# The first level's c·x product of the delta-rule inverse: 32 matmuls of 32x32 in place of 16 of 64x32

## The chip, the cores and the metric

The kernel runs on one NeuronCore of a Trainium2 chip. TensorE (PE in the rows) multiplies, VectorE (DVE) and ScalarE (ACT) do the elementwise work, SyncE (SP) issues nearly all transfers. The metric is the device time of one execution in microseconds; smaller is better.

## What is computed

Two transformer-like blocks on 256 tokens of width 1024, in float32. The first block projects its normed input to four mixers (softmax attention with a forget gate, gated delta rule, and two gated linear attentions), then runs a convolutional gated feed-forward; the second block adds a short convolution mixer, a differential attention and two more feed-forwards. The change lies in the gated delta rule, which solves with a unit lower triangular matrix of 64x64 for each of 4 heads x 4 chunks:

```python
def gated_delta_chunked(q, k, v, g, beta):
    ...
    m = jnp.where(strict, jnp.einsum('bhnrd,bhnsd->bhnrs', kb, k) * decay, 0.0)
    t_mat = m + jnp.eye(c, dtype=m.dtype)
    w = lax.linalg.triangular_solve(t_mat, kb * jnp.exp(G)[..., None],
                                    left_side=True, lower=True, unit_diagonal=True)
    u = lax.linalg.triangular_solve(t_mat, v * beta[..., None],
                                    left_side=True, lower=True, unit_diagonal=True)
    ...
```

## The kernel before

**How the matrices lie.** There are 16 triangular matrices (4 heads, 4 chunks of 64 tokens). Two chunks stand above each other on the 128 partitions, so a tile such as `mt_gd` or `c_t` is [128, 8, 64]: 8 units `u`, each with two 64x64 matrices (`rows_of_chunk(c)`, L373). The inverse is built in blocks: `inv` and `inv_t` are [128, 8, 32] and hold, for each of the four `QUARTERS` of 32 partitions (L382), one 32x32 diagonal block of the inverse and of its transpose.

**How the inverse grows.** `gdn_first_inverse` (L2412) and `gdn_first_turned` on VectorE write the inverse of the 2x2 blocks. Then five levels `lv` = 0 to 4 double the block size: 4, 8, 16, 32 and 64. For each level VectorE makes `c_t` by multiplying `mt_gd` with the mask of that level (`packed(lv + 1)`, L2425 and L2438): at level 0 this leaves entries only inside 4x4 blocks on the diagonal. `gdn_cx(lv)` (L971) multiplies `c_t` with `inv` into PSUM bank 2; ScalarE copies the product to `y_gd` (L1706); `gdn_xcx(lv)` (L981) multiplies `y_gd` and `inv_t` both ways into banks 6 and 0 by `block_products` (L964), which takes 8 units x 4 quarters of 32x32; VectorE subtracts the results from `inv` and `inv_t` (L2445). At level 4 the product joins the two halves of 64 and has a form of its own.

**What sets the order.** All engines run orders written out by hand. On TensorE (L1216 to L1220) the two products of each level are separated by a quarter of a projection (`quarter(*fills[...])`), 12 matmuls of 128x256 that need nothing of the inverse, so that the copies of ScalarE and VectorE lie beside them:

```python
            for lv in range(5):
                gdn_cx(lv)
                quarter(*fills[2 * lv])
                gdn_xcx(lv)
                quarter(*fills[2 * lv + 1])
            gdn_solve()
```

Matmuls of this part are issued by the helper `mm` (L534), those of the projections by `add` (L583). One float32 matmul of L534 in the program shows as two MATMUL records in the trace and two weight loads: the 16 of `gdn_cx` as 32 and 32, the 64 of `block_products` twice as 128 and 128.

**The weights** stream through a ring of three buffers (`raw`, split by ScalarE at L1477 into `w_hi`, by VectorE at L2220 into `w_lo`); SyncE refills a buffer when it has been split. The rest of the program (feed-forwards with a hardware loop of 4 rounds each, attention) comes after and isn't touched.

Of the kernel before, what the change touches and what calls it, by code (L numbers as in the profile page):

```python
# [121 lines left out]
def build(nc, weights, small_in, x_in, masks_in, ident_in, channel_in, row_in, w_gk_in, p_in, table_in,  # L122
# [4 lines left out]
    with ExitStack() as ctx:  # L127
        sems = {}

        def sem(name):  # L130
            if name not in sems:
                sems[name] = ctx.enter_context(nc.semaphore(name))
            return sems[name]
# [36 lines left out]
        def place(shape):  # L170
            n = int(np.prod(shape[1:]))
            at = arena["at"]
            arena["at"] += n
            assert arena["at"] <= ARENA, arena
            v = arena_store[0:shape[0], at:at + n]
            if len(shape) == 3:
                v = v.rearrange("p (a b) -> p a b", a=shape[1])
            elif len(shape) == 4:
                v = v.rearrange("p (a b c) -> p a b c", a=shape[1], b=shape[2])
            return v  # L180
# [49 lines left out]
        c_t = place([P, 8, CHUNK])  # L230
        ngd_tri = place([P, 8, CHUNK])
        HALF = CHUNK // 2
        two_blocks = lambda v: [b.rearrange("p u n -> p (u n)").rearrange("p (u n) -> p u n", n=HALF) for b in (v[:, 0:4, :], v[:, 4:8, :])]
        inv, inv_t = two_blocks(dec)
# [139 lines left out]
        def rows_of_chunk(c):  # L374
            return slice(c * CHUNK, (c + 1) * CHUNK)
# [6 lines left out]
        QUARTERS = [slice(HALF * q, HALF * (q + 1)) for q in range(4)]  # L382

        def block_at(b, u, rows):

            return PS[rows, b, u * HALF:(u + 1) * HALF]
# [145 lines left out]
        def _(pe):  # L532
            def mm(o, lhs, rhs, start=True, stop=True):
                return pe.matmul(o, lhs, rhs, start=start, stop=stop)  # L534
# [436 lines left out]
            def gdn_cx(lv):  # L971

                pe.wait_ge(sem("inv_ready"), lv + 1)
                pe.wait_ge(sem("ct_ready"), lv + 1)
                for u in range(8):
                    for c in range(2):
                        r = rows_of_chunk(c)
                        last = mm(block_at(2, u, r), c_t[r, u, :], inv[r, u, :])
                last.then_inc(sem("cx"), 1)
# [236 lines left out]
# [5 lines that stand above are left out]
# [2192 lines left out]
```

## Time and profile before

| | |
|---|---|
| time, median of 3 runs | 1030.57 us (1029.82 to 1030.59) |
| the profiled execution | 1031.03 us, its span 1029.2 us |
| TensorE matmul busy | 1006.5 us, 98% of the span |
| VectorE busy | 845.6 us, 82% |
| ScalarE busy | 621.4 us, 60% |
| TensorE share of the chain that ended last | 87% |
| granted TensorE clock, mean | 0.998 |
| the stretch from the first `gdn_cx` to the end of the last `gdn_xcx` | 68.97 to 95.6 us |

The page gives each engine's busy time over the span; the chain that ended last gives, followed back from the last instruction, what each step waited for. The clock stood at its upper level (2.4 GHz) in the whole stretch of the change. Instructions are counted as they were executed, the loops' rounds each time.

### The profile page before, as it was taken

The page shows a single profiled execution, that of the slowest core. Times are in us where ns is not written, and L with a number is a line of the kernel's source. Part 1 is how long each engine was busy: PE and PEld are TensorE (multiplying, and loading weights), DVE is VectorE, ACT ScalarE, POOL GpSimd, SP SyncE. Part 2 cuts the span into 40 slices and gives each one's busy share as a digit, 9 for nine tenths or more (in the row PEclk, how much of TensorE's full clock was granted, in tenths as well). Part 3 has the DMA queues.
Part 4 walks back from the last instruction along what each step waited for, and adds up shares of the span by engine and source line. Part 5 has one row for each costly group of instructions (what it writes and reads, how often), then busy time and mean ns, then how long its engine had stood idle before and what let it go on. Part 6 is the DMA issues. An engine that isn't in the chain of part 4 may idle for free.

```text
span 1029.2 us, 21310 instructions
## 1 busy us (share of the span) xinstructions
PE 1006.5 (98%) x8589; PEld 941.0 (91%) x8589; DVE 845.6 (82%) x1211; ACT 621.4 (60%) x856; POOL 5.8 (1%) x16
## 2 busy tenths in 40 slices
PE   7999999999999999999999999999999999999996
PEld 6999889998999999899999999998999999999985
DVE  5964797699988878878999888799775899988876
ACT  6754555566655655556665555666576666555665
POOL 0000000000000000000000000000000000000000
PEclk9999999999999999999999999999999999999999
DMA  8533223455655544566556555444434355655531
GB/s 325 181 100 110 83 85 123 149 193 194 215 188 184 199 163 166 178 232 219 185 205 216 186 204 169 159 164 164 159 130 144 126 202 197 212 187 185 199 123 41
DMA packets 26500, 176.02 MB, mean 171 GB/s; under 512 B 3229, under 2 KB 3509, under 8 KB 6080
## 3 DMA queue, kind: packets, MB, share of 16 engines
q1 hardware_dynamic: 25616, 171.31, 47.8%
q0 software_dynamic: 816, 3.73, 1.1%
q8 instruction: 52, 0.85, 0.3%
q14 instruction: 16, 0.13, 0.0%
HBM read 173.97 MB, written 2.63 MB: 172 GB/s over the span
## 4 chain that ended last, share of the span: by engine, by line
PE 87%; DVE 6%; ACT 3%; DMA 2%; issue 1%; SPq 0%; DVEq 0%; ACTq 0%
PE PS L583 74%; PE PS L534 13%; DVE w_lo L2220 2%; ACT w_hi L1477 1%; DMA arena<-masks_in 1%; DMA raw<-weights 1%; PE PS L1385 0%; DVE h_store L3145 0%; DVE arena L2357 0%; DVE arena L2617 0%; DVE h_store L2233 0%; DVE act_lo L2233 0%; DVE arena L2766 0%; DVE x L2770 0%; PE PS L801 0%
## 5 line engine op out<-in xcount | busy, mean ns | idle before, releaser
L583 PE MATMUL PS<-h_store,w_hi 128*128 128x512 f32 (+1 forms) x1808 | 482.9, 342 | 10.3 <-DVE w_lo L2272 7.5
L2220 DVE TENSOR_TENSOR w_lo<-raw,w_hi 128x2048 fp32r<-128x2048 f32 x156 | 357.1, 2290 | 58.0 <-ACT w_hi L1477 52.8
L583 PE MATMUL PS<-h_store,w_lo 128*128 128x256 f32 (+1 forms) x1384 | 373.3, 282 | 0.0
L583 PEld LDWEIGHTS PS<-h_store,w_hi 128*128 128x128 f32 x1808 | 305.7, 188 | 51.7 <-DVE w_lo L2272 7.8
L1477 ACT ACTIVATE w_hi<-raw 128x2048 fp32r<-128x2048 f32 x156 | 297.8, 1910 | 75.7 <-PE PS L583 60.7
L583 PEld LDWEIGHTS PS<-h_store,w_lo 128*128 128x128 f32 (+1 forms) x1384 | 256.5, 189 | 0.8 <-issue 0.6
L583 PE MATMUL PS<-act_hi,w_hi 128*128 128x256 f32 x704 | 196.4, 281 | 0.2
L583 PE MATMUL PS<-act_hi,w_lo 128*128 128x256 f32 x704 | 195.4, 279 | 0.0
L583 PE MATMUL PS<-act_lo,w_hi 128*128 128x256 f32 x704 | 192.1, 279 | 0.0
L583 PEld LDWEIGHTS PS<-act_hi,w_hi 128*128 128x128 f32 x704 | 132.5, 188 | 2.9 <-issue 1.3
L583 PEld LDWEIGHTS PS<-act_hi,w_lo 128*128 128x128 f32 x704 | 132.5, 188 | 0.0
L583 PEld LDWEIGHTS PS<-act_lo,w_hi 128*128 128x128 f32 x704 | 130.6, 188 | 0.0
L1904 ACT ACTIVATE arena<-PS 128x512 f32<-128x512 f32 x51 | 30.2, 592 | 87.3 <-PE PS L583 87.3
L1896 ACT ACTIVATE arena<-arena,channel 128x256 f32<-128x256 f32 x132 | 63.7, 531 | 22.4 <-DVE arena L2919 15.6
L583 PE MATMUL PS<-w_hi,h_store 128*128 128x256 f32 (+1 forms) x352 | 76.7, 307 | 0.0
L2896 DVE SCALAR_TENSOR_TENSOR arena<-arena,channel 128x254 f32<-128x254 f32 x132 | 57.9, 480 | 7.6 <-DVE arena L2892 0.3
L583 PEld LDWEIGHTS PS<-w_hi,h_store 128*128 128x128 f32 x352 | 57.7, 188 | 3.5 <-issue 0.4
L2892 DVE SCALAR_TENSOR_TENSOR arena<-arena,channel 128x255 f32<-128x255 f32 x132 | 57.7, 479 | 3.8 <-ACT arena L1896 3.8
L583 PE MATMUL PS<-w_lo,h_store 128*128 128x256 f32 (+1 forms) x176 | 52.5, 301 | 0.0
L2917 DVE TENSOR_TENSOR arena<-PS,arena 128x512 f32<-128x512 f32 x51 | 35.0, 687 | 20.6 <-ACT arena L1904 20.6
L534 PE MATMUL PS<-h_store,w_hi 128*128 128x256 f32 x288 | 51.3, 280 | 0.1
L534 PE MATMUL PS<-arena 32*32 32x32 f32 (+7 forms) x1548 | 45.0, 222 | 1.2 <-issue 0.4
(365 smaller groups left out, 1118.9 us busy)
## 6 DMA issues: line engine op xcount, KB each, us to landing
raw<-weights SPq DMA_DIRECT2D x155, 1024.0 KB, 4.9
raw<-weights SPq DMA_DIRECT2D x12, 256.0 KB, 3.6
arena<-masks_in SPq DMA_DIRECT2D x1, 1600.0 KB, 12.1
bias_by_key<-bias_by_distance POOLq DMA_DIRECT2D x1, 1536.0 KB, 9.0
x<-x_in SPq DMA_DIRECT2D x4, 256.0 KB, 4.5
raw<-weights SPq DMA_DIRECT2D x2, 512.0 KB, 9.2
arena<-bias_by_key POOLq DMA_DIRECT2D x1, 1024.0 KB, 6.7
result<-arena SPq DMA_DIRECT2D x4, 256.0 KB, 2.1
```

The source lines that it names most:

```text
L534: return pe.matmul(o, lhs, rhs, start=start, stop=stop)
L583: return pe.matmul(o, lhs, rhs, start=start, stop=stop, skip_group_check=True)
L1477: act.activation(w_hi[:, slot, :], raw[:, slot, :], ACT.Copy).then_inc(hi_ready, 1)
L1896: ins = act.activation(dst[:, c, :], src[:, c, :], ACT.Identity, scale=w, bias=b)
L1904: act.activation(low, PS[:, bank:bank + 2, TOK:512], ACT.Copy).then_inc(sem("low_copied"), 1)
L2220: tt(w_lo[:, slot, :], raw[:, slot, :], w_hi[:, slot, :].bitcast(F), ALU.subtract).then_inc(lo_ready, 1)
L2892: stt(y[:, c, 1:TOK], src[:, c, 0:TOK - 1], channel[:, bass.ds(col(1) + c, 1)], y[:, c, 1:TOK], ALU.mult, ALU.add).then_inc(ready[0], 1)
L2896: ins = stt(y[:, c, 2:TOK], src[:, c, 0:TOK - 2], channel[:, bass.ds(col(0) + c, 1)], y[:, c, 2:TOK], ALU.mult, ALU.add)
L2917: tt(z, PS[:, bank:bank + 2, 0:TOK], low, ALU.add).then_inc(sem("parts_added"), 1)
```

## The change

In `gdn_cx`, level 0 alone takes a branch of its own. Where the code before multiplies, for each unit and each chunk, a 64x64 `c_t` with the 64x32 stack of two `inv` blocks (64 rows contracted, 64 output partitions, 32 columns), the new code multiplies for each unit and each quarter the 32x32 diagonal block of `c_t` with the 32x32 block of `inv` (32 rows contracted, 32 output partitions, 32 columns). `at` picks the columns of `c_t` that belong to the quarter. What is left out are products with the off-diagonal 32x32 blocks of `c_t`, which are zero at this level. Destination, semaphores and waits are the same; levels 1 to 4 are the same.

```diff
@@ -973,6 +973,11 @@
                 pe.wait_ge(sem("inv_ready"), lv + 1)
                 pe.wait_ge(sem("ct_ready"), lv + 1)
                 for u in range(8):
+                    if lv == 0:
+                        for i, r in enumerate(QUARTERS):
+                            at = slice(HALF * (i % 2), HALF * (i % 2) + HALF)
+                            last = mm(block_at(2, u, r), c_t[r, u, at], inv[r, u, :])
+                        continue
                     for c in range(2):
                         r = rows_of_chunk(c)
                         last = mm(block_at(2, u, r), c_t[r, u, :], inv[r, u, :])
```

TensorE's program at this place, between the last projection matmuls before the product and the first ones after it; `w_hi`, `w_lo` and `h_store` are a projection's, `arena` holds `c_t` and `inv`:

```order
@@ -312,6 +312,6 @@
 L583 MATMUL PS<-w_lo,h_store 128x256
 L583 MATMUL PS<-w_hi,h_store 128x256
-L534 MATMUL PS<-arena 64x32 [waits ct_ready,inv_ready]
-L534 MATMUL PS<-arena 64x32 x15
+L534 MATMUL PS<-arena 32x32 [waits ct_ready,inv_ready]
+L534 MATMUL PS<-arena 32x32 x31
 L583 MATMUL PS<-w_hi,h_store 128x256
 L583 MATMUL PS<-w_lo,h_store 128x256
```

Nothing else moves; everything that TensorE's program holds after this place stands 16 matmuls, with their weight loads, further back in it. The other engines' programs are the same but for line numbers.

## Rows read from the trace of the kernel before

**Rows 1.** The page: span, busy time and share of each engine.
```profile
span 1029.2 us, 21310 instructions
...
PE 1006.5 (98%) x8589; PEld 941.0 (91%) x8589; DVE 845.6 (82%) x1211; ACT 621.4 (60%) x856; POOL 5.8 (1%) x16
```

**Rows 2.** The page: chain that ended last, shares of the span.
```profile
PE 87%; DVE 6%; ACT 3%; DMA 2%; issue 1%; SPq 0%; DVEq 0%; ACTq 0%
```

**Rows 3.** The chain by time, 64 to 100 us: start us, us, engine and line.
```profile
71.70 1.16 PE PS L534 x79
72.86 0.40 issue
73.26 0.28 PE PS L534 x9
...
85.21 0.53 issue
85.74 1.09 PE PS L583 x8
...
98.93 0.59 ACT arena L1692
```

**Rows 4.** PE in order of time: start us, us, line, operation, records [idle before].
```profile
68.97 1.12 PE L534 MATMUL PS<-arena 64*64 64x32 f32 x32
70.02 0.39 PE L583 MATMUL PS<-w_hi,h_store 128*128 128x256 f32 x1
...
71.63 1.23 PE L534 MATMUL PS<-arena 32*32 32x32 f32 x119
73.26 0.28 PE L534 MATMUL PS<-arena 32*32 32x32 f32 x9 [0.40 <-issue]
```

**Rows 5.** Windows of L534 on PE: us, busy (records), clock, DMA share, GB/s.
```profile
68.97:70.02 1.05, 1.05 (x32) 1.00 0.00 0
...
80.58:81.63 1.05, 1.05 (x32) 1.00 0.30 117
...
92.28:93.33 1.05, 1.05 (x32) 1.00 0.02 8
77.73:78.97 1.24, 1.24 (x128) 1.00 0.01 0
83.23:84.47 1.24, 1.24 (x128) 1.00 0.43 139
89.43:90.67 1.24, 1.24 (x128) 1.00 0.00 0
```

**Rows 6.** DVE and ACT beside levels 0 and 1, in order of time.
```profile
67.29 0.69 DVE L2425 TENSOR_TENSOR arena<-arena 128x512 f32<-128x512 f32 x1 [3.22 <-ACT arena L1692]
...
69.87 0.43 DVE L2433 TENSOR_TENSOR arena<-arena 128x256 f32<-128x256 f32 x1
70.21 2.29 DVE L2220 TENSOR_TENSOR w_lo<-raw,w_hi 128x2048 fp32r<-128x2048 f32 x1
...
73.59 0.42 DVE L2445 TENSOR_TENSOR arena<-arena,PS 128x256 f32<-128x256 f32 x1 [0.16 <-PE PS L534]
...
70.14 0.38 ACT L1706 ACTIVATE arena<-PS 128x256 f32<-128x256 f32 x1 [0.94 <-PE PS L534]
```

**Rows 7.** The page: the queue of instruction transfers, packets and MB.
```profile
q8 instruction: 52, 0.85, 0.3%
```

**Rows 8.** Windows, all engines: us, PE, PEld, DVE, ACT, POOL, clock, DMA share, GB/s.
```profile
70.42:71.88 1.46, 1.46 (x40) 1.33 (x43) 1.46 (x1) 1.46 (x2) 0.00 (x0) 1.00 0.06 11
75.04:76.03 0.99, 0.99 (x33) 0.95 (x32) 0.10 (x1) 0.00 (x0) 0.00 (x0) 1.00 0.06 17
...
73.25:85.73 12.48, 11.95 (x381) 11.12 (x382) 7.08 (x11) 5.49 (x10) 0.00 (x0) 1.00 0.36 108
...
90.90:92.12 1.22, 1.22 (x12) 1.22 (x11) 1.22 (x4) 0.00 (x0) 0.00 (x0) 1.00 0.55 181
...
293.34:326.72 33.38, 33.38 (x227) 30.88 (x226) 28.37 (x35) 19.44 (x23) 0.00 (x0) 1.00 0.55 188
```

## The prediction

> **What bounds the kernel now.** I read the page first: TensorE is busy for 98% of a span of 1029.2 us [rows 1] and has 87% of the chain that ended last [rows 2]. So what shortens TensorE's own work shortens the kernel, and a wait taken off another engine brings nothing. Next I read the chain by time around the change. From 68.97 to 98.9 us it never leaves TensorE, where ScalarE takes it over at 98.93 [rows 3]; up to there a microsecond off TensorE's row is a microsecond off the chain. In it stand two entries "issue", 0.40 us at 72.86 and 0.53 us at 85.21, where TensorE waits for no other engine [rows 3]. They turn out to be larger than, or as large as, all that the change can gain, so they have to be understood too.
>
> **The product itself.** Before, it is 32 records of 64x32 from 68.97, and the next matmul starts at 70.02: 1.05 us, 32.8 ns a record [rows 4, 5]. The trace has the new form already, in the other product of the levels: 128 records of 32x32 with four quarters in the same order take 1.24 us, 9.7 ns a record, three times the same [rows 5]. The new product is 64 such records: 64 x 9.7 ns = 0.62 us. Gain: 1.05 - 0.62 = 0.43 us. Twice as many instructions cost nothing of their own, since the 9.7 ns already hold a weight load for each matmul. The ends are 0 (64 records at half of 32.8 ns) and 0.43; I take 0.43, because the row is of the same shape, count per unit and bank layout.
>
> A row could speak against it: all four quarters write one PSUM bank, where before two row tiles did. In the 1.24 us rows four quarters also write one bank (6, then 0), so these traces show no price for it [rows 5]. The Trainium skill says otherwise (TensorEngine Tiling (Array Packing), Gotcha 1: PSUM Pressure): "Different row tiles cannot access same PSUM bank simultaneously". By that rule the quarters would go one after another and the gain would shrink or turn round; it is a rival below.
>
> **Who waits for the product.** Its result goes to ScalarE's copy, 0.38 us at 70.14 [rows 6], and comes 0.43 us earlier. The product behind it, from 71.63, needs this copy (ready 70.5) and VectorE's result of L2433 (69.87 + 0.43 = 70.30) [rows 4, 6]. Pulled to 71.20 it still finds both, with 0.7 us to spare. Its own results go to VectorE, which is held by the 2.29 us split at 70.21 until 72.4 and reads the second one at 73.59 [rows 6]; the next user on TensorE comes only at 75.08, after 12 projection matmuls. Inputs of the changed product: `c_t` is written at 67.29 + 0.69 = 67.98, a microsecond before use, and is unaffected [rows 6]. No engine is late by this. SyncE's refills follow the splits, which no one moves. So by the matmuls alone the answer is -0.43 us.
>
> **What the 32 more instructions move.** All later code of TensorE stands 64 records further back in its program (32 MATMUL and 32 weight loads). The two "issue" stalls look like waits for code. First, there is a queue of instruction transfers with 52 packets and 0.85 MB, 16.3 KB each [rows 7]. In windows with nothing else on the DMA engines one read is seen: 11 GB/s x 1.46 us = 16 KB from 70.42 to 71.88, and 17 GB/s x 0.99 us = 17 KB from 75.04 to 76.03 [rows 8]. Second, between the restarts after the stalls, 73.26 and 85.74, TensorE ran 381 + 382 = 763 records and some five waits [rows 8]: 768 = 3 x 256. The whole agrees: 2 x 8589 records [rows 1], less nine repeated loop rounds of 453 [rows 8], over 52 packets, is 252 a packet. So I read: code comes in blocks of 256 instructions, the next block is fetched when one is entered, and a block that is run through faster than a fetch takes ends in a stall. This stretch is the fastest in instructions of the program: a run of 256 records in 1.24 us, against 24 in 1.4 us for a projection quarter.
>
> The Trainium skill has this (Runtime: NRT & Kernel Launch, Instruction fetch mechanics: refills in 16 KiB blocks of 256 instructions, the next fetched while the current one is executed), and calls the cost of crossing a border mostly hidden. The two rows of 0.40 and 0.53 us show it unhidden here; by the page's rule alone there would be no such term and the time would be that of the first rival.
>
> **Where the borders fall.** The restart at 73.26 has 9 of the 128 matmuls left [rows 4], so this border stands 238 records into the first 256-record product. Before, the one ahead of it was reached at 70.4, just behind the changed product. After, each border stands 64 records earlier in the code. Counting 256 at a time through the known order (24 records a projection quarter, 64 a `gdn_cx`, 256 a `gdn_xcx`, a wait or two between), with 4.85 ns a record in the products of 32x32 and 16.4 ns in those of 64x32 [rows 5], the times at which TensorE would reach them are:
> - 71 records into the changed product, 68.97 + 0.34 = 69.31; then 174 into the first `xcx`, 71.63 + 0.84 - 0.43 = 72.04. Block length 2.73 us.
> - 59 into the second `xcx`, 77.73 + 0.29 = 78.02 (length near 6, harmless); then 34 into the third `cx`, 80.58 + 0.56 = 81.14. Length 3.12.
> - 201 into the third `xcx`, 83.23 + 0.97 = 84.20. Length 3.06.
> - 86 into the fourth `xcx`, 89.43 + 0.42 = 89.85 (length 5.6, harmless); then 61 into the fifth `cx`, 92.28 + 1.00 = 93.28. Length 3.43.
>
> The sum of the four short ones is 12.34 us. Before, there were two short ones: 70.4 to 72.86, and 83.3 (9 records into the third `xcx`) to 85.21.
>
> **How long a fetch takes from the border.** From start of read to restart: 73.26 - 70.42 = 2.84. From border to start of read there are two kinds. Where the border follows slow matmuls, or a wait, the read starts with it (70.42 against 70.4); in the midst of a burst or after a stall it starts late: 90.90 [rows 8] against a border at about 90.1, and 75.04 against the restart at 73.26. So from border to usable: 2.47 us (83.27 to 85.74) and 2.9 (70.36 to 73.26) seen as stalls, 0.8 + 1.22 + 1.38 = 3.4 built from the read at 90.90, whose read lasts 1.22 and where 73.26 - 71.88 = 1.38 is what lies behind a read, and 1.78 + 0.99 + 1.38 = 4.2 after a restart. The new short blocks begin in bursts, so I take 3.5, and 3.7 for the third, which follows a stall: 14.2 - 12.34 = 1.9 us of stalls, in place of 0.93. Net of the stalls +0.9, net of all +0.9 - 0.43 = **+0.5 us**. The bounds: with 2.9 everywhere only the first block has a shortfall, 0.17, and the sum is -0.43 - 0.93 + 0.17 = -1.2; with 4.0 it is 16 - 12.34 - 0.93 - 0.43 = +2.3. All three feed-forward loops show equal rounds, so I leave them out. Behind 98.9 us I carry the difference through whole, since TensorE stays the bound.
>
> The sum against the profiled execution is 1031.03 + 0.5 = 1031.5 us; that execution is 0.46 above the median of 1030.57, so the median becomes **1031.1 us**. From no change a measurement here can tell about 0.2%, 2.06 us; even the likeliest case lies deep within that.
>
> **The rivals.**
> - *The borders cost the same*: the reads run early enough, or the stalls have another cause that stays in place. Then only the product counts, -0.43, 1030.1 us. For it: the two stalls seen came at 2.5 to 2.9 us from their border, quicker than my 3.5. Against: stalls of the same size would need the same phase. If the stalls went altogether, it is -1.2 to -1.36, 1029.3 us. Chance 0.38 in all.
> - *Row tiles exclude each other in one bank*: the price of a record stays 32.8 ns, so 64 x 32.8 = 2.1 us, +1.05, 1031.6 us. Against it are the rows of 9.7 ns. Chance 0.03.
> - *Slower, by the code fetch*: every short block costs from its border what the one at 73.26 seems to, 4.2 us. Then 16.8 - 12.34 - 0.93 - 0.43 = +3.1, 1033.7 us. It decides, against the 2.06 us, from (12.34 + 0.93 + 0.43 + 2.06)/4 = 3.94 us a block. For it: the read at 75.04. Against: the four other reads seen. Chance 0.05.
> - *The change does nothing*, as when 32x32 records gain nothing over 64x32 for being half as many: 0, 1030.6 us. Chance 0.04.
>
> **How the numbers follow.** The forecast has 0.50: 1031.1, its own range 1030.4 to 1032.2. The range for 8 in 10 takes in the first rival's far end: 1029.4 to 1032.3. Faster by over 0.2% needs under 1028.5 us, which no case gives: 0.02. Slower needs over 1032.6: the third rival and the tail of the forecast, 0.06. Within: 0.92.
>
> **What would show it.** In the changed kernel's trace: 64 records of 32x32 from 68.97 lasting 0.62 us (right) or over 1.0 (the bank). "issue" stalls no longer behind record 238 of the first `xcx` but behind 174, and not at 85.2 but in the third `cx` and the third `xcx`; stalls 0.4 and 0.5 at the old places would refute the code blocks. The first `gdn_solve` matmul, at 97.2 before, tells the net. The prediction is wrong if that moves by under -0.6 or over +1.6, or if the end moves otherwise than it.

## The result, and the profile after

| | before | changed |
|---|---|---|
| median of 22 runs, taken in turn | 1030.58 us (1029.44 to 1032.18) | 1031.97 us (1030.77 to 1035.0) |
| ratio, 95% interval | | 1.0017 (1.0011 to 1.0023) |
| the profiled execution | 1031.03 us, span 1029.2 | 1032.99 us, span 1031.2 |

The change makes the kernel slower by 1.4 us by the medians, 1.75 us by the ratio (0.17%, an interval of 1.1 to 2.4 us). The forecast was +0.5: the right side, and less than half of the size. The profiled execution is 1.0 us slower than the median of its kind, so its rows show the effect larger than it usually is.

The product does nearly what was said of it. These are the windows of L534 in the changed kernel (us, busy, records, clock, DMA share, GB/s), to be laid beside [rows 5]:

```profile
68.27:68.95 0.68, 0.68 (x64) 1.00 0.00 0
76.91:78.15 1.24, 1.24 (x128) 1.00 0.23 66
```

From the start of the product to the next projection matmul it is 0.68 us in place of 1.05: 0.37 gained, where 0.43 was forecast. The difference of 0.06 is the tail of a burst, which 64 records carry as 128 do. The trace of before had this number too: its product of level 4 is 64 records of 32x32, and its window (same columns) is

```profile
94.94:95.62 0.68, 0.68 (x64) 1.00 0.83 253
```

And this is TensorE in order of time, for [rows 4], the product and all lines of it with idle time before them, and what stands just ahead of those (the view ends at 100.4, inside the last line):

```profile
68.27 0.75 PE L534 MATMUL PS<-arena 32*32 32x32 f32 x64
...
70.56 0.94 PE L534 MATMUL PS<-arena 32*32 32x32 f32 x87
72.16 0.56 PE L534 MATMUL PS<-arena 32*32 32x32 f32 x41 [0.66 <-issue]
...
79.75 0.71 PE L534 MATMUL PS<-arena 64*64 64x32 f32 x17
80.63 0.65 PE L534 MATMUL PS<-arena 64*64 64x32 f32 x15 [0.17 <-issue]
...
82.81 1.08 PE L534 MATMUL PS<-arena 32*32 32x32 f32 x100
84.83 0.44 PE L534 MATMUL PS<-arena 32*32 32x32 f32 x28 [0.94 <-issue]
...
92.32 1.11 PE L534 MATMUL PS<-arena 64*64 64x32 f32 x30
94.29 0.24 PE L534 MATMUL PS<-arena 64*64 64x32 f32 x2 [0.86 <-issue]
...
98.37 1.26 PE L534 MATMUL PS<-arena 64*64 64x64 f32 x38
100.32 0.29 PE L534 MATMUL PS<-arena 64*64 64x64 f32 x4 [0.69 <-issue]
```

The stalls stand where the count of 256 instructions put them: behind 87 matmuls (174 records), 17 (34), 100 (201) and 30 (61), with a fifth in the solve products. Before there were two, 0.40 and 0.53 us [rows 3]. The count holds everywhere: with all of TensorE's records counted from the first one of the program (matmuls, weight loads, and the waits and branches of its sequencer), the number of records ahead of a restart is a multiple of 256 and 193 or 194 more. That is so for every wait of TensorE on "issue" of over 0.1 us from the first product to the linear attention, 48 of them in the 18 profiles of this case. All TensorE's waits of the stretch, in one line of the view of waits, 64 to 101 us (engine and line, waited for: us, times, longest):

```profile
PE PS L534 <- issue: 3.3, 5, 0.9
```

To compare profiles I use two measures of my own from the start times of the matmuls: *the stretch*, from the projection matmul just ahead of the first `cx` to the 1620th matmul of the kernel before (in the linear attention, 110.98 us), and *the pauses*, the distances between successive starts in it that exceed 0.3 us, without one of 0.31 that all have. Behind that matmul the rest takes 909.6 to 910.3 us in all profiles but one, with or without the change (910.9 in the changed kernel with cut transfers), so that part is the same. The start of the stretch varies: the changed kernel's profile reached it at 68.06 us, that of before at 68.76, by nothing that the change touches. This is why the two spans differ by 2.0 us and the two stretches by 2.8.

| profile | stretch, us | pauses, us |
|---|---|---|
| before | 42.22 | 0.59 + 0.81 = 1.40 |
| changed | 45.03 | 0.85 + 0.39 + 1.13 + 1.08 + 0.91 = 4.36 |

2.96 more of pauses less 0.37 for the product is 2.59, of 2.81 measured. There is one profile of before, and two more of the changed kernel, below, have far smaller pauses; so a difference between two single profiles says where time goes, and not how much of it the median loses.

### The profile page after: what moved, and what is told of

It is laid out like the page before. It is cut to its first block, busy times and chain, and to the rows that moved or that the text cites. A ratio compares the mean times of both kernels' runs of the same rounds, so it can differ in the third digit from the quotient of the medians.

```text
span 1031.2 us, 21374 instructions
## 1 busy us (share of the span) xinstructions
PE 1006.4 (98%) x8621; PEld 940.2 (91%) x8621; DVE 845.4 (82%) x1211; ACT 621.6 (60%) x856; POOL 5.8 (1%) x16
## 4 chain that ended last, share of the span: by engine, by line
PE 87%; DVE 6%; ACT 3%; DMA 2%; issue 1%; SPq 0%; DVEq 0%; ACTq 0%
PE PS L583 74%; PE PS L534 13%; DVE w_lo L2225 2%; ACT w_hi L1482 1%; DMA arena<-masks_in 1%; DMA raw<-weights 1%; PE PS L1390 0%; DVE h_store L3150 0%; DVE arena L2362 0%; DVE arena L2622 0%; DVE h_store L2238 0%; DVE act_lo L2238 0%; DVE arena L2771 0%; DVE x L2775 0%; PE PS L801 0%
## 5 line engine op out<-in xcount | busy, mean ns | idle before, releaser
L534 PE MATMUL PS<-h_store,w_hi 128*128 128x256 f32 x288 | 51.3, 280 | 0.1
L534 PE MATMUL PS<-arena 32*32 32x32 f32 (+6 forms) x1580 | 45.3, 221 | 4.2 <-issue 3.3
```

## The experiments

**The borders alone.** If it is the place of the code that matters, the kernel before must lose without the new product. The first way used instructions that raise a semaphore:

```diff
+            for _ in range(64):
+                pe.sem_inc(sem('pad'), 1)
             first_columns()
```

> The kernel before, its product unchanged, with 64 instructions that do nothing for the computation (each raises a semaphore that nobody reads) at the start of TensorE's program, where it waits some 7 us for the first inputs. All code behind them stands as far back as in the changed kernel. Theory A (code arrives in blocks of 256 instructions, and the blocks' borders decide): the stalls of the changed kernel without its product: behind 87 of 128 records of the first xcx, 17 of 32 of the third cx, 100 of 128 of the third xcx, 30 of 32 of the fifth cx and in the solve products, 3.0 to 4.4 us in sum in place of 1.4 (start to start), so 1.5 to 3 us slower than before in the profile and +1.8 us (1.2 to 2.5) in the median. Theory B (something about the 32x32 product itself makes the later work late): stalls stay at 119 of 128 and behind the third xcx, and the time is that of before within 0.4 us.

Measured: the stalls moved. The chain of this kernel in order of time (start us, us, what):

```profile
82.75 0.64 PE PS L534 x17
83.39 0.46 issue
83.85 0.65 PE PS L534 x15
...
86.10 1.01 PE PS L534 x69
87.11 0.67 issue
87.78 0.44 PE PS L534 x25
```

Behind 17 of 32 and 100 of 128 records, the changed kernel's places, with the product untouched; none at 119 of the first `xcx` any more. But only two of the five: pauses 1.54, not 3.0 to 4.4; stretch 42.52. The time, 1034.05 against 1030.26 us, is mostly the start: the first matmul came at 10.74 us, not 7.49, since each of these instructions takes some 150 ns (from 128 to 192 of them, below, the first matmul moves by 9.8 us). The 0.5 us left is less than the 1.2 to 2.5 expected. Theory A has the places and not the sizes; theory B has neither.

The same with 16 matmuls of 32x32, 64 records, which are done long before the first input:

```diff
+            pe.wait_ge(*once("zeros"))
+            for i in range(16):
+                r = QUARTERS[i % 4]
+                mm(PS[r, 3, 0:HALF], zeros_r[r, 0:HALF].bitcast(F), zeros_r[r, 0:HALF].bitcast(F))
             first_columns()
```

> The kernel before with 16 matmuls of 32x32 on zeros (64 records) at the very start of TensorE's program, while it waits for its first inputs; they take 0.3 us there and delay nothing, unlike the semaphore instructions that cost 150 ns each. Theory A (borders): stalls at the changed kernel's places, no other difference to before; the profile from the first cx to matmul 1620 between 42.5 (as with 64 semaphore instructions) and 44.7 us, before 42.2; time +0.3 to +1.5 us. If the time is within 0.2 us of before, the phase alone costs nothing and the loss comes from the product's burst.

Measured: first matmul of the kernel proper at 7.19 us, pauses 0.81 and 0.85 at the same two places, stretch 42.64. The median is 1032.73 against 1030.20 us, ratio 1.0026 (1.0013 to 1.0038). More was lost than the 0.3 to 1.5 us expected, 2.5 by the medians (interval 1.3 to 3.9), so about as much as by the change itself or more, in a kernel that has every product as before. Its profiled execution, 1031.29, is the fastest of its six, so the profile shows too little of it; where the other five lost their time isn't seen.

**Back to the old places.** 192 semaphore instructions in the changed kernel, and as controls 128 and 192 in the kernel before:

> The changed kernel with 192 such instructions at the start of TensorE's program: 64 + 192 = 256, so that the borders of blocks fall where they fell before. Theory A: the product at 0.68 us as in the changed kernel (1.05 before), stalls again behind 119 of 128 records of the first xcx and in the projection behind the third xcx, 0.4 and 0.5 us and slightly longer for the 0.37 us that comes earlier; time -0.4 to +0.3 us against before. Should the 192 instructions take longer than the 7 us of waiting at the start, the first matmul is late by it and that is to be taken off. Theory B: as slow as the changed kernel, +1.4 to +1.8 us.

> The kernel before with 128 such instructions: a phase between. Theory A: borders stand behind 55 of 128 records of the first xcx, 110 records (55 matmuls less) earlier in the levels, stalls at other places than in either kernel (in the middle of the second and fourth xcx); their sum between 1 and 4 us, so time -0.4 to +3 us. Theory B: the time of before within 0.4 us.

> The kernel before with 192 such instructions, the control for the 192 of the changed kernel's version: what they cost at the start shows in the first matmul's time. Theory A: stalls at yet other places (third cx and xcx of other levels), sum 1 to 4 us. Theory B: the time of before within 0.4 us.

Measured, the chain of the changed kernel with 192:

```profile
93.41 1.16 PE PS L534 x78
94.57 1.88 issue
96.45 0.28 PE PS L534 x9
...
107.74 0.67 PE PS L583 x4
108.41 1.31 issue
109.72 1.09 PE PS L583 x8
...
122.83 0.80 PE PS L1049 x6
123.64 1.06 issue
124.69 0.44 PE PS L1049 x2
```

The first two are exactly the places of [rows 3], 9 matmuls and 8 projection matmuls ahead of the next piece. Their sizes are not: 1.88 and 1.31 in place of 0.40 and 0.53, and a third has come. The part "borders back, loss back" fails. Medians (1055.47, 1046.52, 1057.51 us) say nothing, since the padding delayed the start to 30.3, 20.5 and 30.3 us. With 128 and 192 in the kernel before, the pauses were 3.01 and 4.20, stretch 43.66 and 45.12: with the old product too, these phases look worse than the one that the kernel before happens to have. These are single profiles, and one and the same kernel ranges from 1.26 to 4.36 (the changed one, below).

**The changed kernel at other phases**, with matmuls as padding, as in the diff above, 16, 32 and 48 of them:

> The changed kernel with the same 16 matmuls at the start: all borders 64 records earlier than in the changed kernel. By block lengths of the changed kernel three blocks are short (2.7, 1.5 and 2.4 us), and at 3.6 to 4.2 us a block the stalls sum to 4.1 to 5.9 us: 1 to 2 us slower than the changed kernel, +2 to +4 us against before. Without theory A: no difference to the changed kernel.

> The changed kernel with 32 such matmuls (128 records) at the start. Short blocks by the changed kernel's lengths: four of 2.9 to 3.25 us, stalls 2.0 to 4.4 us in sum: near the changed kernel, +0.5 to +2.5 us against before.

> The changed kernel with 48 such matmuls (192 records) at the start: 64 + 192 = 256, so borders at the places in the code where they were before, and no late start as with the semaphore instructions. Stalls behind 119 of 128 records of the first xcx, in the projection behind the third and perhaps in the solve. Theory A as first put (the phase of before gives back before's stalls): -0.4 to +0.3 us. As the run with 192 semaphore instructions suggests (the read starts later behind the faster product): stalls 3.2 to 5 us in sum, +1.5 to +3 us.

| padding of the changed kernel, records | ratio to before (interval) | stretch, us | pauses, us |
|---|---|---|---|
| 0 | 1.0017 (1.0011 to 1.0023) | 45.03 | 4.36 |
| 64 | 1.0018 (1.0008 to 1.0027) | 41.81 | 1.53 |
| 128 | 1.0045 (1.0027 to 1.0064) | 43.36 | 2.81 |
| 192 | 1.0014 (1.0003 to 1.0025) | 43.86 | 3.41 |

Again the places held (with 192: 1.63 us idle ahead of 9 matmuls, 1.30 ahead of 8 projection matmuls). With 64 the expectation was too high: 4.1 to 5.9 us of stalls and +2 to +4 us, against 1.53 and +1.6 by the medians. With 128 it was too low: +0.5 to +2.5 us, against +3.3. With 192 the first form of theory A (-0.4 to +0.3) fails, and the median, +1.5, stands at the low end of the second form. The profiles with 64 and 128 are the fastest of their ten and six executions, so they show too little, and the two right columns don't rank the phases. None of the four phases of the changed kernel is as fast as the kernel before. Why the old places cost more with the new product is seen at the first border: it falls 6 or 7 records behind it. In the kernel before the read of the next block began within 0.1 us of TensorE's reaching the border [rows 8]; behind the faster product it began 1.37 and 1.38 us after. TensorE's records then came at three times the rate. The other traces go with this (those with doubled transfers, below, left aside). At the border in or just behind the product, the read began 0.7 to 1.4 us late in all eight profiles in which 71 or more records of the new product had run ahead of it (the three of the changed kernel, cut transfers, even code, four levels, and both with 192 of padding). It began within 0.2 us in the five without: before, before with 64 of padding in both forms, before with cut transfers, and the changed kernel with 64, where the border falls only 7 records into the new product. The last one differs from the changed kernel in its padding alone. How the burst delays the read isn't shown.

**More of the same.** The edit is one line:

```diff
-                    if lv == 0:
+                    if lv < 4:
                         for i, r in enumerate(QUARTERS):
```

> The changed kernel with the product in 32x32 tiles at all of the levels 0 to 3, not at level 0 alone (at these levels too the off-diagonal 32x32 blocks that are left out are zero). By the matmuls alone it takes off 4 x 0.37 = 1.5 us against before, 1.1 against the changed kernel. Theory A: it adds 192 more records, so that a level is 432 records in some 5.1 us, 256 in 3.0 us, below what a block costs (3.5 us and more): the stretch becomes bound by code reads. Stretch from the first cx to the solve: 8.2 blocks at 3.6 to 4.2 us = 29.5 to 34 us against 28.3 before; +1 to +5 us against before. If the bank were the reason of any loss, its record pitch in the levels would be well over 9.7 ns.

Measured: 1036.12 against 1030.14 us, ratio 1.0056 (1.0040 to 1.0073), a little above the range expected. The four products are each 0.37 us shorter, 1.5 in all, and the kernel is 6 us slower. The chain:

```profile
76.62 1.21 PE PS L534 x81
77.83 2.44 issue
80.28 0.32 PE PS L534 x3
...
91.07 0.77 PE PS L534 x55
91.84 1.40 issue
93.24 0.66 PE PS L534 x45
```

The stretch from the first `cx` to the solve was 31.7 us against 28.3, inside the expected 29.5 to 34; the records kept their pace, 64 in 0.68 us and 128 in 1.24. This is the clearest run for theory A: with more instructions for less work the kernel is slower. Part of it is the clock, below.

**Even code.** The projection matmuls in pieces of 6, 12 and 6:

```diff
-                quarter(*fills[2 * lv])
-                gdn_xcx(lv)
-                quarter(*fills[2 * lv + 1])
+                eighth(*fills[2 * lv], 0)
+                gdn_xcx(lv, lambda: (eighth(*fills[2 * lv], 1), eighth(*fills[2 * lv + 1], 0)))
+                eighth(*fills[2 * lv + 1], 1)
```

> The changed kernel with the projection matmuls between the products dealt out finer: 6 ahead of the first 64 matmuls of an xcx, 12 between its two halves, 6 behind, in place of 12 and 12; the same instructions, no data of the one needed by the other. Theory A: code runs more evenly, every block of 256 takes 3.4 to 4.4 us of work; stalls shrink to under 2.5 us in sum, so -1 to -2 us against the changed kernel, if the 6 matmuls (0.7 us) still cover ScalarE's copy of 0.38 us; if they don't, 0.1 to 0.3 us a level are given back. A theory in which the stalls have nothing to do with the rate of instructions: no gain.

Measured: the stalls are gone; from 68 to 99 us the chain has one "issue" entry left, in front of these matmuls (0.23 us from start to start):

```profile
81.36 0.01 issue
81.37 0.65 PE PS L534 x15
```

The blocks took 3.71 to 4.34 us each. The stretch is 42.15 us, which is that of before, and the median 1031.21 against 1030.14, ratio 1.0011 (1.0001 to 1.0020): by the medians 0.8 us less than the changed kernel, but the intervals of the two ratios overlap, so the gain is likely and not shown. The 1 to 2 us expected did not come, and it is not faster than before. What it gives back is the price of changing between 128x128 matmuls and small tiles. Going in there are 0.21 us between starts; coming out 0.12 to the first projection matmul and 0.22 from it to the second, where projection matmuls stand 0.12 apart and records of 32x32 0.01. Two pieces of 6 projection matmuls take 1.82 us where one of 12 took 1.61, and two of 64 small ones 1.36 where one of 128 took 1.24. That is 0.3 us for each of the four levels in which the finer order has one more such pair, 1.3 us, about what the stalls had cost.

**Weight traffic.** The trace records when each read of 16 KB began and ended. In the changed kernel:

| border reached, us | read began | weights arrived | block usable |
|---|---|---|---|
| 68.57 | 69.46 (+0.89) | none | 72.15 (+3.58) |
| 77.14 | 77.92 (+0.78) | 76.3 to 77.7 | 80.63 (+3.49) |
| 80.63 | 82.44 (+1.81) | 79.4 to 80.8 | 84.84 (+4.21) |
| 89.83 | 91.58 (+1.75) | 90.3 to 91.6 | 94.29 (+4.46) |
| 94.29 | 98.13 (+3.84) | 93.4 to 94.8, 95.1 to 98.6 | 100.32 (+6.03) |

In the last three blocks the read began late, in the last two within 0.5 us of the end of a transfer. From the read's end to the next start of a matmul it was 1.24 to 1.51 us in all five. A window in that last wait shows what filled the DMA engines (columns as in [rows 8]: 0.97 of their time, 339 GB/s):

```profile
95.10:98.10 3.00, 3.00 (x84) 2.83 (x84) 0.65 (x2) 0.00 (x0) 0.00 (x0) 1.00 0.97 339
```

So the transfers of blocks 9 to 14 were cut in both kernels (the rest of each buffer keeps older data, so the mixers compute with other numbers), then doubled in both. In both forms blocks 12 and 13 came whole:

```diff
-                sp.dma_start(raw[:, n % RING, :], weights[n - 1]).then_inc(raw_loaded[n % RING], 16)
+                w = 32 if 9 <= n <= 14 else BLK
+                sp.dma_start(raw[:, n % RING, 0:w], weights[n - 1][:, 0:w]).then_inc(raw_loaded[n % RING], 16)
```

> The changed kernel with the transfers of weight blocks 9 to 14 cut to 32 of their 2048 columns (the rest of each buffer keeps older data, so the mixers and projections compute with other numbers; every instruction is as before, and blocks 12 and 13 come in one transfer, not four). It takes nearly all weight traffic out of 70 to 105 us. Theory C (the read of a code block queues behind weight traffic): each read starts within 1.4 us of its border, where 1.8, 2.2 and 3.8 us were seen in the changed kernel; blocks are usable 3.2 to 3.8 us after the border, the stalls at the same five places sum to 1 to 2.3 us (start to start) in place of 4.4, and the time is 2 to 3 us below the changed kernel's, near 1029.5. Theory D (the delay of the reads has nothing to do with weights): stalls sum to about 4.4 again and the time is 1032.

> The kernel before with the same cut in the transfers of weight blocks 9 to 14 (other numbers in the mixers, same instructions). Theory C: its two stalls began without traffic at their reads (read 0.06 us after and 0.38 us before the border), so they stay at 1.4 us in sum within 0.5; time 1030 to 1030.6, and against it the changed kernel with the cut gives the change without contention: -0.4 to +0.7 us. Theory D: the same for this kernel, but +1.4 to +2 us for the change.

```diff
+                if 9 <= n <= 14:
+                    sp.dma_start(raw[:, n % RING, :], weights[n - 1]).then_inc(sem("twice"), 16)
+                    twice[0] += 1
+                    sp.wait_ge(sem("twice"), 16 * twice[0])
                 sp.dma_start(raw[:, n % RING, :], weights[n - 1]).then_inc(raw_loaded[n % RING], 16)
```

> The changed kernel with the transfers of weight blocks 9 to 14 each made twice, the second when the first has landed (12 and 13 whole, not in four pieces): twice the weight traffic in some 70 to 105 us, same instructions on TensorE. Theory C (the reads of code queue behind weights): reads start later, stalls from the first cx to matmul 1620 sum to 4.5 us or more (2.6 with little traffic, 4.7 in the changed kernel's profile); time 1 us or more above the changed kernel's, 1032.5 to 1035, unless weights themselves come late (then TensorE's idle time shows VectorE's or ScalarE's split as the end of a wait). Theory E (the loss is the burst and the borders, traffic only scatters single executions): time within 0.7 us of the changed kernel's 1032.

> The kernel before with the same doubled transfers, the control. Theory C: less affected, since its two stalls follow reads that start outside of traffic; +0 to +1 us (1030.2 to 1031.2). If it loses as much as the changed kernel's version does, the traffic costs both alike and says nothing of the change.

| weight transfers 9 to 14 | before: median | pauses | changed: median | pauses | difference of medians |
|---|---|---|---|---|---|
| cut | 1030.23 | 0.86 | 1031.49 | 2.27 | 1.26 |
| as they are | 1030.58 | 1.40 | 1031.97 | 4.36 | 1.39 |
| doubled | 1033.95 | 5.16 | 1040.23 | 7.16 | 6.28 |

The pauses are of one profile each. The 2.27 with cut traffic lies among the 4.36, 2.40 and 1.26 of the changed kernel as it is, so it is no evidence; the starts of the reads are. With the traffic cut no read in the stretch began later than 1.44 us after its border in the changed kernel, where each of its three profiles with full traffic has one of some 2 us or more (3.84, 1.99 and 2.20). With it doubled they began 3.08, 3.42, 2.29 and 3.83 us after it, at 72.13, 93.61, 98.36 and 104.58, and the transfers ended at 72.2, 93.6, 98.7 and 104.7. The other two that fell to a time of transfer, at 76.36 and 109.24, also began in its last half microsecond; the two with no transfer, at 83.75 and 87.88, began 0.7 and 1.4 us after their border. No wait for weights appears in either doubled kernel (all of TensorE's idle time there ended on "issue"), so the loss is not a late weight.

That a code read waits for weights is shown by this. But theory C claimed the changed kernel's loss for it, and that falls: without the traffic 1.26 us of difference stays, outside the -0.4 to +0.7 expected, and the changed kernel with cut transfers took 1031.49 us, not the 1029.5 expected. Of the stalls of before, 0.86 us stayed, a little under the 1.4 within 0.5. The doubled kernels lost more than expected (1032.5 to 1035 and 1030.2 to 1031.2). The doubled pair has medians of 4 and 6 runs only, and part of the loss is the clock, below. Also 1.8 of the 7.16 and 0.7 of the 5.16 are not stalls but the ordinary distances between pieces, which at half clock exceed 0.3 us.

**The changed kernel twice more.**

> The changed kernel as it is, for a second profile. In 22 executions it took 1030.8 to 1035.0 us. Theory: borders at the same five places; what varies is when each read starts. If the time is near 1031, the reads in blocks ending in the fifth cx and in the solve start within 1.3 us of their border and one or both of those stalls (1.08 and 0.91 us in the first profile) are gone; stalls and time move together, everything before the first cx and behind matmul 1620 within 0.5 us.

> The same once more, for a third profile of the changed kernel: as for the second. The stalls' sum, less 0.4 us for the product and less 1.7 us for the stalls of before, should give the difference in the stretch from the first cx to matmul 1620 (42.2 us before) within 0.3 us in each of the three profiles.

Measured: 1031.44 us with a stretch of 43.14 and pauses of 0.77 + 1.14 + 0.49 = 2.40; 1031.21 us with 41.88 and 0.67 + 0.59 = 1.26. The chain of the second:

```profile
72.87 0.48 issue
73.34 0.56 PE PS L534 x39
...
84.69 0.40 issue
85.09 0.44 PE PS L534 x25
```

The places are those of the first profile; the fourth and fifth pause, 1.08 and 0.91 there, are gone here, with reads that began 0.77 and 1.88 us after their border in place of 1.75 and 3.84. The second profile misses the expectation in part: near 1031 us, it keeps 0.49 at the fourth. So does the third, whose first matmul came 1.0 us later than the first profile's; its time, 1031.21, hides how short its stretch is. Taking 42.22 - 1.40 - 0.37 = 40.45 and adding the pauses gives 44.81, 42.85 and 41.71 for stretches of 45.03, 43.14 and 41.88: 0.2 to 0.3 below in each.

## Why the prediction was wrong

- **The product** (0.43): right in kind, 0.37; the 0.68 us of 64 records stood in the trace of before (94.94), and I scaled from 128 instead. Its records kept their pace with four quarters in one bank. The rule quoted from TensorEngine Tiling (Array Packing), Gotcha 1, of the Trainium skill, which would have made it slower, isn't borne out here: 0.68 us, not over 1.0.
- **Nobody else waits**: right. All of TensorE's idle time from 64 to 101 us in the changed kernel ended on "issue", none on ScalarE or VectorE.
- **Blocks of 256 instructions**: right, four of four places to the record, and the four blocks without stalls add up to 12.34 us, as forecast. The first rival, in which the borders cost the same, is refuted by its own test. The Trainium skill (Runtime: NRT & Kernel Launch, Instruction fetch mechanics) gives the block's size, and these places agree with it; its "mostly hidden" does not hold for this stretch, with 3.3 us of such idle time in the first profile.
- **How long a block takes**: this is the step that failed, by its size. I took one length for all, 3.5 us three times and 3.7 once, 14.2 us for the four. The first profile had 3.58, 3.49, 4.21 and 4.46, 15.7 in all; the second 14.8, the third 13.5. What varies is when the read begins. I had 0.8 us behind a border in a burst and 1.8 after a restart [rows 8], and used the first for nearly all; in these three profiles it was 0.74 to 3.84 us, the long ones after a stall or under weight traffic. Against the lengths without pauses that makes 3.4 us of stalls in the first profile and 2.3 in the mean of three, not 1.9.
- **A block that the sum left out**: I stopped counting at the border in the fifth `cx`. The block behind it, 5.1 us of work, ends in the solve. In the first profile it took 6.03 us, because its read began 3.84 us late: 0.9 us more. In the other two it cost nothing. I had a row for a wait of 1.78 after a restart and none beyond it; and I left out that weights run at 95 to 99 us.
- **What a stall costs**: "issue" rows count idle time only. From start to start the two of before cost 0.59 and 0.81, not 0.40 and 0.53; beyond the usual distances of 0.01 and 0.12, 1.27 us, not 0.93. This alone went the other way.
- With these terms the sum is 4.30 - 1.27 - 0.37 = +2.7 for the first profile (measured 2.8). In the mean of the three it is 2.34 + 0.30 - 1.27 - 0.37 = +1.0 (measured 1.1), where the median moved by 1.4. The three lie 2.8, 0.9 and -0.3 from the one profile of before; the 0.4 us between their mean and the median is within what so few can tell. The range held the median; the middle was too near to zero. A mechanism that gives +2.8, +0.9 and -0.3 does not fix the sign of a forecast of +0.5; that it was right is in part luck.
- The sign that I had set, the first `gdn_solve` matmul at 97.2, came at 98.4, 97.7 and 97.6: +1.1, +0.5 and +0.3, inside my -0.6 to +1.6. In the first profile it misleads: the first `cx` had come 0.7 us earlier than before, so the levels took 1.85 us longer, and the stall in the solve lies behind that matmul.
- The slower rival, every short block at 4.2 us and decisive from 3.94, gave 1033.7: too dark for the median, though single runs reached 1035.0. It had the right mechanism, and the first profile's four blocks average 3.94.

How the 1.4 us of the median divides between faster arrival at the borders and the moved borders isn't settled: the moved borders alone cost 2.5 us in one comparison of medians (16 matmuls of padding in the kernel before) and 0.3 to 0.4 in the two profiles of before with 64 records of padding. One part is the product's own: the pause in the first `xcx`, 0.85, 0.77 and 0.67 us in the three profiles of the changed kernel, is absent in those two, which have the border at the same place. That is more than the 0.37 us that the product saves. Nor is it settled why the reads begin late where no weights run, as 1.81 us at 80.63.

## What to carry to other kernels

Where TensorE runs small tiles, count its instructions as well as its time: a stretch that uses up 256 of them faster than the next block arrives (mostly 3.4 to 4.5 us here, 2.2 to 6.0 at the ends) waits for its own code, and taking a third off the time of a product by doubling its instructions can make the kernel slower, as four levels of it did by 6 us. Look for "issue" in the chain, count records between such stalls, and before believing a gain of a few tenths of a microsecond in such a stretch, shift the code behind it with padding where the engine idles anyway: if that alone moves the time as much as the edit, the edit wasn't what was measured.

## What the runs showed of the hardware that I had not expected

**Code reads wait for weights.** See above: with doubled transfers, read starts at 72.13, 93.61, 98.36 and 104.58 us, each within 0.4 us of the end of a transfer, up to 3.8 us behind the border.

**Behind four of the stalls the clock fell.** In the changed kernel with doubled transfers TensorE stood still from 72 to 74.4 us (2.40 us idle), and what followed ran at half clock (columns as in [rows 8], clock ahead of the DMA share):

```profile
73.20:74.30 1.10, 0.00 (x0) 0.00 (x0) 0.00 (x0) 0.00 (x0) 0.00 (x0) 0.79 0.92 223
74.40:83.00 8.60, 8.60 (x121) 8.02 (x125) 3.38 (x4) 3.05 (x6) 0.00 (x0) 0.50 0.58 217
101.10:104.50 3.40, 3.40 (x76) 3.18 (x76) 0.00 (x0) 0.31 (x1) 0.00 (x0) 0.51 0.86 308
```

The granted clock is at its lower level, 1.2 GHz, for 8.6 us although TensorE is busy throughout. It fell again just behind two shorter stalls, of 0.67 us before 96.07 and 1.07 us before 100.75. By the two windows at half clock some 6 us of work are lost (an estimate: half of 8.6 and of 3.4). It was the same in two other profiles, for some 3 us each: with the product at four levels (2.44 us idle) and, in the kernel before with doubled transfers (1.95 us idle), here:

```profile
73.40:75.30 1.90, 0.06 (x7) 0.00 (x0) 0.62 (x2) 0.00 (x0) 0.00 (x0) 1.00 0.55 151
75.41:78.70 3.29, 3.29 (x24) 3.00 (x25) 1.55 (x2) 0.00 (x0) 0.00 (x0) 0.50 0.53 222
```

Behind the stall of 1.88 us (the changed kernel with 192 instructions of padding) the clock stayed up, so the length of the last stall alone does not decide it. Its window of 96.5 to 99.9 shows this:

```profile
96.50:99.90 3.40, 3.40 (x57) 3.18 (x58) 2.01 (x3) 0.46 (x2) 0.00 (x0) 1.00 0.35 94
```

So where code falls far behind, the loss can be more than the stall. Whether the slowest executions of the changed kernel, up to 1035.0 us, had this, no profile shows.
